# Expert jobs beside mixers weigh by halves of 64 rows, and their value gathers hold two tokens with 64 experts each

## What is computed

```
q = (hc @ p['w_q']).reshape(chunk, PEER_HEADS, 2, PEER_HALF)
s = jnp.einsum('thcd,hcnd->thcn', q, p['sub_keys']).astype(jnp.float32)
s1, i1 = lax.top_k(s[:, :, 0], PEER_TOPK)
s2, i2 = lax.top_k(s[:, :, 1], PEER_TOPK)
...
best, pos = lax.top_k(cand, PEER_TOPK)
eidx = jnp.take_along_axis(cidx, pos, axis=-1)
gw = jax.nn.softmax(best, axis=-1)
u = jnp.take(p['peer_u'], eidx, axis=0)
act = jax.nn.gelu(jnp.einsum('td,thkd->thk', hc, u).astype(jnp.float32), approximate=False) * gw
v = jnp.take(p['peer_v'], eidx, axis=0)
return jnp.einsum('thk,thkd->td', act.astype(hc.dtype), v)
```

## Time and profile before

| what | us |
|---|---|
| median of 3 runs (5279.08 to 5311.70) | 5279.18 |
| the profiled execution | 5297.07 |
| its span in the trace | 5295.1 |
| first job, units 1 to 8 with the stages between | 627.1 |
| norm stage, first job | 39.3 |
| `choose_experts` of the tokens, layer 0 | 171.2 |
| second job, units 1 to 8 with the stages between | 567.8 |
| `finish_experts` | 300.3 |

### The profile page before, as it was taken

How to read it: one execution, slowest core, us unless ns; L and a number is a source line. 1 busy time by engine, 2 the same in 40 slices (tenths; PEclk the granted TensorE clock), 3 DMA queues, 4 the chain that set the end, 5 groups by cost and what they waited for, 6 DMA issues and landing times. The chain is left out here.

```text
span 5295.1 us, 87998 instructions
## 1 busy us (share of the span) xinstructions
PE 3740.9 (71%) x36238; PEld 2819.0 (53%) x36238; DVE 2454.9 (46%) x5650; ACT 1087.5 (21%) x2789; POOL 1706.1 (32%) x1745
## 2 busy tenths in 40 slices
PE   7989896976767886765645599988430325877788
PEld 6777684864545563654421187776300001766677
DVE  2756547675553264774450023663968240143310
ACT  1234311232222111342310022442100000111300
POOL 0000003245564244465566500000567776000000
PEclk9999997987787897886767799998765667888899
DMA  5423246777786587677789743003799999312242
GB/s 210 132 94 130 89 151 260 263 239 253 270 273 237 213 333 289 228 251 256 271 318 368 301 140 115 3 3 108 287 360 350 362 362 345 124 59 62 88 142 105
DMA packets 298909, 1117.72 MB, mean 211 GB/s; under 512 B 33681, under 2 KB 39073, under 8 KB 289953
## 3 DMA queue, kind: packets, MB, share of 16 engines
q0 software_dynamic: 221184, 805.40, 42.5%
q1 hardware_dynamic: 77344, 306.90, 16.9%
HBM read 1111.13 MB, written 1.05 MB: 210 GB/s over the span
## 5 line engine op out<-in xcount | busy, mean ns | idle before, releaser
L2135 POOL DMA_INDIRECT ring<-in_peer_u,expert_number x624 | 720.4, 1154 | 1204.8 <-DVE expert_number L2446 566.4
L2092 DVE CUSTOM_DVE_ANT_0 ring<-ring,tok 128x1024 f32<-128x1024 f32 x624 | 754.8, 1225 | 482.7 <-DMA ring<-in_peer_u,expert_number 454.8
L2118 PE MATMUL psum<-spare,picked 128*32 128x512 f32 x1472 | 283.2, 870 | 520.5 <-issue 241.5
L2118 PEld LDWEIGHTS psum<-spare,picked 128*32 128x32 f32 x1472 | 60.2, 138 | 737.0 <-issue 736.6
L2149 POOL DMA_INDIRECT spare<-in_peer_v,expert_turned x368 | 352.3, 957 | 157.1 <-issue 92.9
L177 PE MATMUL psum<-h,weight_ring 128*128 128x256 f32 x1728 | 386.0, 387 | 22.6 <-PEq L96 22.6
L177 PEld LDWEIGHTS psum<-h,weight_ring 128*128 128x128 f32 x1728 | 336.3, 195 | 71.7 <-issue 23.9
L1823 PE MATMUL psum<-h,weight_ring 128*128 128x256 f32 x1344 | 294.3, 380 | 3.5 <-PEq L96 3.5
L1823 PEld LDWEIGHTS psum<-h,weight_ring 128*128 128x128 f32 x1344 | 254.8, 190 | 41.7 <-issue 7.5
L1339 PE MATMUL psum<-h,weight_ring 128*128 128x256 f32 x1056 | 236.8, 386 | 8.6 <-PEq L96 8.6
L2149 POOL DMA_INDIRECT weight_ring<-in_peer_v,expert_turned x174 | 181.9, 1045 | 139.0 <-PE psum L2118 90.1
(11 more groups left out here) (617 smaller groups left out, 7368.3 us busy)
## 6 DMA issues: line engine op xcount, KB each, us to landing
weight_ring<-in_w_in SPq DMA_DIRECT2D x226, 512.0 KB
ring<-in_ada_w SPq DMA_DIRECT2D x24, 1024.0 KB, 12.0
weight_ring<-in_w_q SPq DMA_DIRECT2D x48, 512.0 KB
weight_ring<-in_ada_w SPq DMA_DIRECT2D x16, 1024.0 KB, 6.5
weight_ring<-in_w_out SPq DMA_DIRECT2D x32, 512.0 KB
gate_ring<-in_w_gate SPq DMA_DIRECT2D x32, 512.0 KB, 3.6
weight_ring<-in_w_mlp_in SPq DMA_DIRECT2D x32, 512.0 KB
weight_ring<-in_w_mlp_out SPq DMA_DIRECT2D x8, 2048.0 KB
```

Of the source, the lines that this page charges most:

```text
L2092: dve.tensor_tensor_reduce(place.rows, place.rows, b.tok[:, tile, :], 1.0, 0.0, ALU.mult, ALU.add, b.dots[:, tile, slot:slot + 1]).then_in ...
L2118: mm = pe.matmul(out, place.window.columns[:, strip, first:first + STRIP], part.rows[:, 512 * half:512 * half + 512], start=(m % BATCHES = ...
L2135: pool.indirect_dma_start(place.rows, None, b.tables["u"], bass.IndirectOffsetOnAxis(ap=b.number[:, r:r + 1], axis=0)).then_inc(place.sem, 16)
```

## The change

A job is cut into four groups of 64 rows (two halves of 64 expert slots for each tile of tokens) in place of two tiles. `weigh_half` weighs a group as soon as its 64 rows are done, and opens its 16 batches. For this a value gather no longer holds 128 experts of one token: it holds 64 experts of one token in partitions 0 to 63 and the same 64 slots of another token in partitions 64 to 127. The expert numbers and the weights are turned by `turn_half` (two matmuls of 64 rows for each 64 columns) in place of a transpose, and the window gets two columns, each zero in one half (`k.halves`), by a TENSOR_TENSOR in place of a COPY. Gather size, gather count, batch count and the matmuls of a batch are unchanged: 256 rows, 64 batches of four gathers. `choose_last` worked that way before; its branch becomes the only one. In `finish_experts` POOL issues the gathers of two more batches before it picks the weights of the first.

```diff
@@ -2017,18 +2017,15 @@
         self.row, self.fetched, self.places, self.turn, self.stage = 0, 0, {}, 0, 0
         self.batch, self.batches_fetched, self.groups = 0, 0, {}
         self.weighed, self.finished, self.consumed, self.weights_kept = 0, 0, {}, {group: None for group in range(GROUPS)}
-        self.tokens = 1
         self.banks = [6, 6]
     def batch_of(self, m):
-        group, c = divmod(m, BATCHES // self.tokens)
-        return group // self.tokens, group, c
+        group, c = divmod(m, PAIRS)
+        return group // 2, group, c
     def open_batches(self):
-        if self.tokens == 2:
-            return PAIRS * self.weighed
-        return BATCHES * min(self.weighed, self.finished + 1 if self.banks[0] == self.banks[1] else 2)
+        return PAIRS * min(self.weighed, 2 * self.finished + 2 if self.banks[0] == self.banks[1] else GROUPS)
 def expert_buffers(k, mem, dram):
...
         (tile, _, c), place = job.batch_of(m), place_batch(k, m)
-        first = STRIP - 1 - job.tokens * c
+        first = STRIP - 1 - 2 * c
         for part in place.parts:
...
@@ -2145,7 +2142,7 @@
-    token = (SLOTS * group + STRIP * strip) // job.tokens + c
+    token = HALF * group + STRIP // 2 * strip + c
...
@@ -2160,14 +2157,9 @@
         pool.wait_ge(*place.free)
     if job.weights_kept[group] is not None:
         pool.wait_ge(*job.weights_kept[group])
-    width = SLOTS // job.tokens
-    weights = job.lists.weights[:, width * group + c:width * group + width:STRIP // job.tokens]
-    if job.tokens == 1:
-        pool.tensor_copy(place.window.columns[:, :, STRIP - 1], weights).then_inc(k.picked.sem, 1)
-    else:
-        shape = [P, STRIPS, 2]
-        pool.tensor_tensor(place.window.columns[:, :, STRIP - 1:STRIP + 1], weights.unsqueeze(2).broadcast_to(shape),
-                           k.halves.unsqueeze(1).broadcast_to(shape), ALU.mult).then_inc(k.picked.sem, 1)
+    weights, shape = job.lists.weights[:, HALF * group + c:HALF * group + HALF:STRIP // 2], [P, STRIPS, 2]
+    pool.tensor_tensor(place.window.columns[:, :, STRIP - 1:STRIP + 1], weights.unsqueeze(2).broadcast_to(shape),
+                       k.halves.unsqueeze(1).broadcast_to(shape), ALU.mult).then_inc(k.picked.sem, 1)
     job.batches_fetched = m + 1
...
@@ -2221,37 +2213,43 @@
-    if job.weighed < 2 and job.row >= SLOTS * (job.weighed + 1):
-        weigh_tile(k, job)
+    while job.weighed < GROUPS and job.row >= HALF * (job.weighed + 1):
+        weigh_half(k, job)
-def weigh_tile(k, job):
-    b, tile = job.shared, job.weighed
+def group_of(t, group):
+    return t[:].rearrange("p t c -> p (t c)")[:, HALF * group:HALF * group + HALF]
+def weigh_half(k, job):
+    b, group = job.shared, job.weighed
+    dots, part = group_of(b.dots, group), slice(HALF * group, HALF * group + HALF)
-            act.activation(b.dots[:, tile, :], b.dots[:, tile, :], ACT.Gelu).then_inc(k.act_step.up(), 1)
+            act.activation(dots, dots, ACT.Gelu).then_inc(k.act_step.up(), 1)
-            act.activation(job.lists.weights[:, SLOTS * tile:SLOTS * tile + SLOTS], k.bank(5, SLOTS), ACT.Copy).then_inc(k.act_step.up(), 1)
+            act.activation(job.lists.weights[:, part], k.bank(5, HALF), ACT.Copy).then_inc(k.act_step.up(), 1)
-            dve.tensor_tensor(b.dots[:, tile, :], b.dots[:, tile, :], b.gw[:, tile, :], ALU.mult).then_inc(k.vec_step.up(), 1)
+            dve.tensor_tensor(dots, dots, group_of(b.gw, group), ALU.mult).then_inc(k.vec_step.up(), 1)
-            pe.transpose(k.bank(5, SLOTS), b.dots[:, tile, :], k.ident).then_inc(k.turned.up(), 1)
+            turn_half(k, pe, k.bank(5, HALF), dots).then_inc(k.turned.up(), 1)
...
@@ -2453,8 +2451,8 @@
-                for t in range(2):
-                    mm = pe.transpose(k.bank(4)[:, P * t:P * t + P], s.expert[:, t], k.ident)
+                for group in range(GROUPS):
+                    mm = turn_half(k, pe, k.bank(4)[:, HALF * group:HALF * group + HALF], group_of(s.expert, group))
...
@@ -2524,39 +2522,36 @@
-                def weighted(tile):
-                    dve.wait_ge(k.act_step.sem, k.act_step.at(2 * todo.index(tile) + 1))
-                    dve.tensor_tensor(b.dots[:, tile, :], b.dots[:, tile, :], b.gw[:, tile, :], ALU.mult).then_inc(k.vec_step.up(), 1)
-                for tile in todo:
-                    use_rows(k, dve, SLOTS * (tile + 1) - job.row)
-                    marks["dots", tile] = k.row_used.count
-                    if tile == 0:
-                        use_rows(k, dve, 4)
-                    weighted(tile)
+                for n, group in enumerate(todo):
+                    use_rows(k, dve, HALF * (group + 1) - job.row)
+                    marks["dots", group] = k.row_used.count
+                    use_rows(k, dve, 4)
+                    dve.wait_ge(k.act_step.sem, k.act_step.at(2 * n + 1))
+                    dve.tensor_tensor(group_of(b.dots, group), group_of(b.dots, group), group_of(b.gw, group), ALU.mult).then_inc(k.vec_step.up(), 1)
-                for tile in todo:
-                    act.wait_ge(k.row_used.sem, marks["dots", tile])
-                    act.activation(b.dots[:, tile, :], b.dots[:, tile, :], ACT.Gelu).then_inc(k.act_step.up(), 1)
-                    act.wait_ge(k.turned.sem, k.turned.at(todo.index(tile) + 1))
-                    act.activation(job.lists.weights[:, SLOTS * tile:SLOTS * tile + SLOTS], k.bank(2 + tile, SLOTS), ACT.Copy).then_inc(k.act_step.up(), 1)
-                    job.weights_kept[tile] = k.act_step.sem, k.act_step.count
+                for n, group in enumerate(todo):
+                    act.wait_ge(k.row_used.sem, marks["dots", group])
+                    act.activation(group_of(b.dots, group), group_of(b.dots, group), ACT.Gelu).then_inc(k.act_step.up(), 1)
+                    act.wait_ge(k.turned.sem, k.turned.at(n + 1))
+                    act.activation(job.lists.weights[:, HALF * group:HALF * group + HALF], k.bank(2 + group % 2, HALF), ACT.Copy
+                                   ).then_inc(k.act_step.up(), 1)
+                    job.weights_kept[group] = k.act_step.sem, k.act_step.count
-                for n, tile in enumerate(todo):
-                    if tile == 1 and job.weighed == 0:
-                        job.weighed = 1
-                        use_batches(k, pe, 1)
+                for n, group in enumerate(todo):
-                    pe.transpose(k.bank(2 + tile, SLOTS), b.dots[:, tile, :], k.ident).then_inc(k.turned.up(), 1)
-                job.weighed = 2
+                    if n >= 2:
+                        pe.wait_ge(*job.weights_kept[group - 2])
+                    turn_half(k, pe, k.bank(2 + group % 2, HALF), group_of(b.dots, group)).then_inc(k.turned.up(), 1)
+                job.weighed = GROUPS
...
@@ -2566,9 +2561,14 @@
                     gather_row(k, pool, r)
                 pool.wait_ge(k.pool_step.sem, k.pool_step.count)
+                waiting = []
                 for m in range(job.batches_fetched, job.batch):
                     for strip in range(STRIPS):
                         gather_part(k, pool, m, strip)
+                    waiting.append(m)
+                    if len(waiting) > 2:
+                        pick_weights(k, pool, waiting.pop(0))
+                for m in waiting:
                     pick_weights(k, pool, m)
         b.slots, k.spare_slots, k.own_slots, k.windows = own, [], False, windows
```

4 lines of the change are left out of this document (2 added, 2 removed).

## The result

The changed kernel takes 5319.6 us (median of 20 runs, 5297.64 to 5338.24), the kernel before 5293.62 in the 20 runs beside it (5272.53 to 5311.70). The ratio is 1.0047, 95% interval 1.0036 to 1.0059: 25 us slower, within the 1% that the prediction called no change. The profiled execution has a span of 5311.1 us against 5295.1, +16.0.

What follows compares the result with a forecast made beforehand. No engine bounds the kernel throughout; stages follow behind barriers, so changes add. Tails give 89.7 us back, the batches' new places ask for 124: +34.1, so the median of 5279.2 becomes 5313 us, range 5265 to 5345.

Steps and rivals of the forecast that it cites:

- The first rival: Value gathers hide in the open units: the four converted units cost 17 us, not 88; 5242 us, chance 0.2.
- The second rival: Too few slots: unit 1's opening +8, unit 8 +8, norm stage turns +6; 5335 us, chance 0.25.
- The third rival: Tails, `finish_experts` or `choose_experts`, do not shrink in full: 15 of 89.7 us stay, 5328 us, chance 0.1.
- Converted units priced by a stage with the same load: Units opening five batches earlier priced from earlier stages so loaded: 83.9 us in the first job; second job's units 3-5 +46.2.
- Held up by turns of gather, wait and use: Open units wait on slot turns, not bandwidth or an engine; DMA share only 0.76 to 0.80.
- Unit 1, 8 us hidden: First job's unit 1: first batch's wait overlaps PE's wait for first unit's work, saving 0 to 11.4 us, 8 taken.
- Weighing: Two more weighing stages in each job, 6 us each within bounds 4 and 7.8: +24 us in all.
- Unit 8: First job's unit 8 gets 8 rows and loses the row ring's lent slots: +4 us, bounds 0 to 11.5.
- Unit 7: First job's unit 7 has two batches for five, at 5.0 us each, and fewer rows: 66 for 81.9 us, -16.
- Norm stage, `choose_experts`, `finish_experts`: Norm stage +23.6 us, two more turns of 11.8; `choose_experts` -43.5, ending with its sorts; `finish_experts` -46.2, 32 transfers fewer.
- The early units: First job's units 1 to 3, now opening five batches each: +50.0 us less 8 hidden in unit 1, +42.

Runs made afterwards that it cites:

- the short gathers: Changed kernel with value gathers in the mixers and `choose_experts` bringing 64 columns of 1024, except the first into each slot, count unchanged: 5404.08 us, one execution.

## Why the prediction was right, and where its steps were not

The forecast was 5313 from a median of 5279.2, +34; measured are +25, and the range and the case (open units cost about what the tails give back, and the rest is loss) held. That the time itself is off by 6.6 us only, 5319.6 for 5313, is luck in part: the median of before is 5293.6 in 20 runs and 14 above the one that the forecast started from. The first rival needed open units below 72 us; the four converted ones took 78.5 to 87.8. It also needed bytes to be what counts, and the short gathers speak against that. The second rival named three terms, and each moved its way: nothing of unit 1's opening was hidden, unit 8 paid 11.6 more than the term (it had 8), and a turn is 13.1 us, between 11.8 and its 14. The total stayed below it since unit 7 and units 6 to 8 of the second job came out lower. Its reason, too few slots, is not borne out: in the second job twelve for eight change nothing, and in unit 8 of the first lent slots made it longer. The third rival did not show: both tails gave back what was forecast, to 2.2 us.

*Converted units priced by a stage with the same load.* Right: units 3 to 5 of the second job +44.2 for +46.2, units 2 and 3 of the first 163.9 for 167.8 (163.9 to 169.9 in all but one of the eight traces with this load, 159.2 in that one). *The reason given was wrong.* "Held up by turns of gather, wait and use" is refuted as far as it rests on few slots or on the bytes of a gather. The price was right since it was taken from a row with the same load, whatever it is in it that costs.

*Unit 1, 8 us hidden.* The prediction let the first batch lie on PE's wait for the first unit's work. It doesn't: the weighing stage with its barrier lies between. PE's timeline, after:

```profile
1134.79 0.48 PE L1980 MATMUL psum<-constants,dots 128*64 128x64 f32 x4 [14.14 <-DVE dots L2247]
1147.42 3.25 PE L2115 MATMUL psum<-weight_ring,picked 128*32 128x512 f32 x16 [12.15 <-DMA weight_ring<-in_peer_v,expert_turned]
```

PE first waits 14.14 us in the weighing stage, as VectorE is not done with its last rows and with the operands of the first unit, and then 12.15 for the first values. Weighing and unit 1 together are 105.9 us; the forecast had 6 + 92.2 = 98.2, and the 7.7 between them are about the 8 that were taken off. In the seven other traces with this load the two take 107.9 to 119.2.

*Weighing.* The step failed where a weighing stage meets a late engine: 18.2 us for 6. The other stages are 4.0 to 7.7, within the bounds of 4 and 7.8. In the second job three stages for one add 11.3.

*Unit 8.* The mis-sized term: +15.6, above its bound of 11.5. The bounds priced only the rows (8.0 measured). The move of `finish_tile` stood at nothing; but it now lies ahead of this unit, and the wait of an opening (14.37) lies in it.

*Unit 7.* -24.8 for -16. The price of 5.0 a batch took no notice of where its gathers are issued. By the counts of the trace before: 28 row gathers (unit 2) take a unit from 35.0 to 58.9, 0.85 each; 23 and 20 value gathers (unit 4) take it to 83.8, which leaves 29.2 for the 20, or 1.46 each. DMA issues by tile in unit 7 after:

```profile
ring<-in_peer_u,expert_number POOLq DMA_INDIRECT x24
x_tokens<-in_peer_v,expert_turned POOLq DMA_INDIRECT x2
y<-in_peer_v,expert_turned POOLq DMA_INDIRECT x1
weight_ring<-in_peer_v,expert_turned POOLq DMA_INDIRECT x1
```

24 and 4 give 35.0 + 20.4 + 5.8 = 61.2. It took 57.1 here and 55.2 to 62.4 in seven other kernels with two batches and 23 rows there (two of them leave other work out), all below the forecast's 66. The same prices give 61.3 for unit 8 before (18 value gathers, no rows; 62.5), 72.1 for unit 8 of the second job after (23 and 12; 71.3) and 66.3 for it with twelve slots (23 and 8; 64.9), units from which they were not taken. They do not hold for unit 8 of the first job after (4 and 20: 67.6 for 78.1), where the opening is added. The count was to be had before. By it, too, 5.8 of the 7.8 us that units 6 to 8 of the second job lost are unit 8, which issues 12 value gathers for 16 (71.3 us for 77.0); the forecast had them at nothing.

*Norm stage, `choose_experts`, `finish_experts`.* 63.2 for 63; 125.5 for 128; 254.4 for 254, at a DMA share still of 0.96. Each had one measured duration that carried it: the turn, the sorts' end, a transfer at the tail's rate. In the norm stage a small miss is hidden: its three turns are 12.1, 13.2 and 13.1 us for 11.8 each, and PE comes to its first batch 2.6 us sooner than before (24.8 us into the stage for 27.4).

The misses of unit 8 (+11.6), unit 7 (-8.8), the early units (-8.4), the first job's weighing (+10.8) and units 6 to 8 of the second job (-7.8) cancel in the sum. The early units and the weighing do so for a reason: PE's wait for the first unit's work lay in unit 1 before and lies in the weighing stage after. For the rest nothing links them, and the total is nearer than its parts by luck.

## What to carry to other kernels

Price a stage that gets more work by a stage of the same trace that has the same load, gathers counted where they are issued and not where they are used. A single buffer before a barrier costs its whole turn for each further use (13.0 us here, against 5.1 for the same batch beside other work): such a stage should get the fewest batches, and with one in place of four there, no difference of the changed kernel from the one before could be told (1.001, 0.9988 to 1.0032). When a schedule is cut finer, list which waits of an opening and which barriers move with it; a new stage exposes whatever engine is late at that point. And read a forecast term against more than one trace: the same units differed by 20 us in sum between traces here.

## What was not expected of the hardware

- Gathers of 128 rows follow each other on POOL at 1.25 us at best, whether they bring 4 KB or 256 bytes a row, and a wait for four of them falls only from 9.8 to 6.7 us when the bytes fall to a sixteenth.
- In bursts of value gathers PE's small matmuls come down from 17 or 18 to 2.4 a us with no semaphore in the way, from six us after the first gather to some 4 us after the last. Such pauses also come with short gathers, at a DMA share of 0.12, and a unit at a share of 0.13 was no faster than one at 0.50.
- Leaving out most of a batch's products lengthened `choose_experts` from 125.5 to 137.4 us (126.3 with short gathers on the same chip), at a granted clock of 0.77 for 0.90, and PE's busy time fell from 103.79 to 90.72 us only. PE stands 23.15 us for VectorE's sorts at the stage's end there (0.69 in the changed kernel), so the time went ahead of the sorts' end. Why was not tried.
